# Softmax probabilities turned two quarters later, and the first two projection units interleaved without GpSimd

## The chip, the cores and the metric

The kernel runs on one core of a Trainium2 chip. The metric is the device time of one execution in microseconds; the median of three runs is compared. The engines are TensorE (PE: matmuls, and PEld: its weight loads), VectorE (DVE), ScalarE (ACT), GpSimd (POOL) and SyncE (SP, which here only issues DMAs).

## The reference

One layer over `x` of 512 tokens by 1024 channels, all in float32:

```python
proj = x @ w_in + b_in                     # 1024 -> 6728 columns, cut into
qa, fa, ia, za, qb, kb, vb, zb, qi, ki, wi, ga, gb = split(proj)
oa = rms_norm(hgrn2(qa, fa, ia)) * g       # gated linear recurrence, 4 heads of 128
# sparse attention, 8 heads of 64:
score = sum_h wi[h] * relu(qi[h] @ ki.T)   # 8 indexer heads, causal
keep  = top 128 keys of each query by score
p  = softmax(qb @ kb.T / 8 + t5_bias, over the kept keys)
ob = p @ vb
merged = sigmoid(ga) * ((oa * silu(za)) @ w_up_a) + sigmoid(gb) * ((ob * silu(zb)) @ w_up_b)
out = layer_norm(alpha * x + merged @ w_out)
```

## The kernel before

Every large product is done with split operands: `a = a_hi + a_lo` with `a_hi` rounded to the fp32r format, and `a*b` as three matmuls, hi·hi, hi·lo and lo·hi (`split_product`). The weights come in units of 256 columns (`UNITS`: kiwi, which holds ki and wi in 72 columns, then qi0, qi1, zb0 and so on up to up3, then four units of `w_out`). Unit u is loaded into `w_raw[:, u % 2]` by SP, rounded into `w_hi` by ScalarE (`split_hi`, two instructions of 128x1024), and subtracted into `w_lo` by GpSimd (`split_lo`, four pieces), or by VectorE for the units in `LO_DVE`, which counts them with a semaphore of its own.

TensorE works through the units in four quarters each. A quarter q = 4u + 0..3 of a normal unit is 12 matmuls of 512 columns (`quarter_f`), or 24 of 256 columns (`quarter_t`, for vb and ia). Two quarters fill one of the two projection banks; ScalarE or VectorE then copies the bank out (`leave_bank`), and TensorE waits for that copy before it fills the bank again a unit later. Behind each quarter every engine runs `side(q)`: the pieces of the token mixers that are due at that quarter. All engines are in-order, each with its program written in the order of q, so the order of all work is the order of these lists.

The softmax attention has 32 items (a block b of 128 queries, and a head), in pairs. `Q_ITEM` says at which quarter an item's scores are computed: quarters 39, 41, ... 53 for the first eight pairs, and 55, 56, 57, 59, 60, 61, 63, 64 for the last eight. For a pair due at q:

- TensorE `scores` in `side(q)` (L479) fills a log bank;
- VectorE `logits` in `side(q)` (L1042) adds the bias and the mask, and writes `prob` and the row maximum `nmax`; behind it in the same `side(q)` come the top-k rounds due then (L1018, L1019; rounds for block 3 are due at quarters 36 to 44), and behind these `invert_sums` (L1053);
- ScalarE `softmax_exp` and `normalise` in `side(q)` (L721, L729), the second waiting for the reciprocal of `invert_sums`;
- TensorE `turn_probs` in `side(q + 1)` (L488) transposes the probabilities; VectorE `move_probs` in `side(q + 1)` (L1030) copies them out; TensorE `attend` in `side(q + 2)` (L504) multiplies them with v; VectorE `gate_group` (L1064) takes a group of four items three quarters after its last item (`Q_GROUP`).

`prob` has two places, so `logits(i)` waits for the transposes of item i - 2.

The opening: ScalarE issues the load of the kiwi weights, then those of the biases and the identity, and rounds kiwi. VectorE makes `x_hi` and `x_lo` for each of the eight slices of x (`split_x`, L929 and L931). GpSimd subtracts kiwi's and unit 1's low parts. TensorE runs all of kiwi (24 matmuls, each slice when its x is there), then all of unit 1 (48). A ScalarE table load stands behind kiwi's copies (L670). SP loads the eight slices of x and then units 1, 2, ...; unit 2 waits until kiwi's low part is done, since they share a place. After the items comes the recurrence ("tree", L539 to L563); its first step on VectorE (`forget(0, 0)`, L1079) stands in `side(68)` behind the gates due by then.

Of the kernel before, what the change touches and what calls it, by code (L numbers as in the profile page):

```python
# [32 lines left out]
P = 128  # L33
# [9 lines left out]
UW = 256  # L43
# [36 lines left out]
Q_GROUP = [Q_ITEM[4 * n + 3] + 3 for n in range(len(GROUPS))]  # L80
# [3 lines left out]
LO_DVE = range(Q_PREP[0] // 4 + 1, Q_MERGE // 4 + 2)  # L84
# [14 lines left out]
def hybrid_kernel(nc, x_t, x_tok, w_units, w_kiwi, b_cols, b_ia, b_vb, lb_cols, g_cols, rel_bias,  # L99
                  ln_g, ln_b, one_hot, ident, causal, tree_masks, out):  # L100
    with ExitStack() as ctx:
# [16 lines left out]
        with ExitStack() as s:  # L118
# [9 lines left out]
            v_b = sb("v_b", [P, TB, D_B], stack=s)  # L128
            t5 = sb("t5", [P, HEADS_B, 2 * P], stack=s)
# [3 lines left out]
            prob = sb("prob", [P, 2, SEQ], stack=s)  # L133
# [33 lines left out]
        with ExitStack() as s:  # L167
# [16 lines left out]
        nmax = sb("nmax", [P, 2])  # L184
# [4 lines left out]
        proj_bank, log_bank, turn_bank, out_bank = ps[0:2], ps[2:4], ps[4:6], ps[6:8]  # L189
        up_bank = log_bank + turn_bank  # L190
# [8 lines left out]
            sem(n) for n in ("k_hi_done", "q_hi_done", "wi_done", "kiwi_out", "k_twice"))  # L199
        consts_in, table_in, row_out, t5_in = sem("consts_in"), sem("table_in"), sem("row_out"), sem("t5_in")  # L200
# [36 lines left out]
        def raw(u):  # L237
            w = unit_width(u)
            return w_raw[:, u % 2, 0:KT * w].rearrange("p (k n) -> p k n", k=KT)

        def split_target(u, over_x, ring):
# [4 lines left out]
            return ring[:, u % 2, :, 0:unit_width(u)]  # L246

        def wait_split_target(eng, u):

            gb3, up2, up3 = (UNITS.index(n) for n in ("gb3", "up2", "up3"))  # L250
            last = {NMAIN: gb3, NMAIN + 1: gb3, NMAIN + 2: up2, NMAIN + 3: up3}.get(u, u - 2)
            if last >= 0:
                eng.wait_ge(part_done, 2 * last + (2 if last else 1))

        def wait_lo(eng, u, n):

            if u in LO_DVE:
                eng.wait_ge(lo_dve, 4 * (u - LO_DVE[0]) + n)
# [87 lines left out]
        def _(sp):  # L346
            for k in range(KT):
                sp.dma_start(x_raw[:, k, :], x_t[:, k, :]).then_inc(x_in[k], 16)
            for u in range(1, NU):
                if u >= 2:  # L350
                    wait_lo(sp, u - 2, 4)
                unit = w_units[u - 1]
                for a in range(2):
                    c = slice(a * KT // 2 * UW, (a + 1) * KT // 2 * UW)
                    sp.dma_start(w_raw[:, u % 2, c], unit[:, c]).then_inc(w_in[u % 2][a], 16)
# [22 lines left out]
        def _(pe):  # L378
# [12 lines left out]
            def wait_bank(u, i):  # L391
                if u == 1 and i == 1:
                    pe.wait_ge(kiwi_out, 1)
# [3 lines left out]
            def quarter_f(u, i, j):  # L397

                bank = proj_bank[1 if UNITS[u] == "kiwi" else i]
                if j == 0:  # L400
                    wait_bank(u, i)
                c = slice(i * P, min(i * P + P, unit_width(u)))
                for k in range(4 * j, 4 * j + 4):
                    if i == 0:
                        wait_piece(u, k)
                    mm = split_product(bank[0:c.stop - c.start, :], w_hi[:, u % 2, k, c], w_lo[:, u % 2, k, c],
                                       x_hi[:, k, :], x_lo[:, k, :], k == 0, k == KT - 1)
                if j == 1:
                    mm.then_inc(part_done, 1)

# [13 lines left out]
            def turn_wi():  # L424
# [6 lines left out]
                mm.then_inc(part_done, 1)  # L431
# [50 lines left out]
            def turn_probs(i):  # L482
# [4 lines left out]
                for c in range(b + 1):  # L487
                    mm = nc.tensor.transpose(turn_bank[i % 2][:, queries(c)], prob[:, i % 2, queries(c)], id_sb[:])  # L488
# [86 lines left out]
            def side(q):  # L575

                if q == 4:
# [25 lines left out]
            for u, name in enumerate(UNITS):  # L603
                for q in range(4):
# [5 lines left out]
                    elif name != "kiwi" or i == 0:  # L610
                        quarter_f(u, i, j)
                    if (u, q) == (1, 3):
# [27 lines left out]
        def _(act):  # L640
            def round_tiles(u, k):
                nc.scalar.activation(split_target(u, x_hi, w_hi)[:, k, :], raw(u)[:, k, :],  # L642
                                     ACT.Copy).then_inc(hi_done, 1)

            def split_hi(u, a):

                if u == 0:
                    act.wait_ge(w_in[0][0], 16)
                else:
                    act.wait_ge(w_in[u % 2][a], 16 * (u // 2 + (a == 0 or u % 2)))  # L650
                if a == 0:
                    wait_split_target(act, u)
                round_tiles(u, slice(4 * a, 4 * a + 4))

            def leave_bank(u, i):
# [5 lines left out]
                act.wait_ge(part_done, 2 * u + i + 1)  # L661
# [837 lines left out]
```

## Time and profile before

| | us |
|---|---|
| median of three runs (509.02 to 511.66) | 510.69 |
| the profiled execution | 510.81 |
| its span, first to last instruction | 508.8 |
| PE busy in it | 479.8 (94%) |
| DVE busy | 294.3 (58%) |
| ACT busy | 206.4 (41%) |
| POOL busy | 187.6 (37%) |

The profiled execution lies 0.12 us from the median, so a sum made on it stands for the median too. Busy PE counts matmuls whose ends are modelled and overlap; the distance from one matmul's start to the next tells more.

### The profile page before, as it was taken

The numbers are of one execution on the slowest core, as the hardware profiler recorded it, in microseconds if no ns is written. First come the engines' busy times: TensorE is split into PE (matmuls) and PEld (weight loads), VectorE is DVE, ScalarE is ACT, GpSimd is POOL, SyncE is SP. The second block draws the span as 40 slices with busy tenths as digits, with TensorE's granted clock in tenths as the row PEclk, the third lists the DMA queues.
The fourth block names the chain that finished last, engine by engine and source line by source line (L and its number), as shares of the span: only waits on it lengthen the run. The fifth ranks groups of instructions, "written<-read, shape, count | busy, mean of one in ns | idle before, by whom it ended". The sixth has DMA issues, their size and how long they took to land. (4 is left out here: it accounts for less than half of the span.)

```text
span 508.8 us, 6785 instructions
## 1 busy us (share of the span) xinstructions
PE 479.8 (94%) x2566; PEld 387.9 (76%) x2566; DVE 294.3 (58%) x552; ACT 206.4 (41%) x343; POOL 187.6 (37%) x170
## 2 busy tenths in 40 slices
PE   4899999999779999999998899989999999999993
PEld 2578888889557888866787787868778888888882
DVE  6634589999773333343379967796352404264276
ACT  2444444323224533454375518545087333343000
POOL 2744433534335533663413200211005555686000
PEclk9899999999898999999999999999999999999998
DMA  8524222233021122112202202012205222348012
GB/s 307 200 85 165 84 83 84 82 107 134 9 83 29 56 84 84 43 41 84 80 4 84 83 1 84 22 63 82 84 0 166 82 84 82 112 166 303 1 62 103
DMA packets 15440, 45.69 MB, mean 90 GB/s; under 512 B 2056, under 2 KB 3504, under 8 KB 15408
## 3 DMA queue, kind: packets, MB, share of 16 engines
q1 hardware_dynamic: 14016, 44.06, 25.5%
q10 hardware_dynamic: 1392, 1.20, 0.7%
q8 instruction: 20, 0.33, 0.3%
q14 instruction: 12, 0.10, 0.1%
HBM read 43.14 MB, written 2.11 MB: 89 GB/s over the span
## 5 line engine op out<-in xcount | busy, mean ns | idle before, releaser
L1355 POOL TENSOR_TENSOR w_lo<-w_raw,w_hi 128x512 fp32r<-128x512 f32 (+1 forms) x104 | 135.2, 1326 | 153.1 <-ACT w_hi L642 153.1
L380 PE MATMUL bank<-x_hi,w_hi 128*128 128x512 f32 (+1 forms) x360 | 147.7, 410 | 9.4 <-POOL w_lo L1355 6.3
L381 PE MATMUL bank<-x_lo,w_hi 128*128 128x512 f32 (+1 forms) x360 | 143.1, 397 | 0.0
L382 PE MATMUL bank<-x_hi,w_lo 128*128 128x512 f32 (+1 forms) x360 | 142.8, 397 | 0.0
L380 PEld LDWEIGHTS bank<-x_hi,w_hi 128*128 128x128 f32 (+1 forms) x360 | 68.7, 191 | 31.7 <-POOL w_lo L1355 7.1
L382 PEld LDWEIGHTS bank<-x_hi,w_lo 128*128 128x128 f32 (+1 forms) x360 | 68.6, 191 | 15.9 <-issue 0.6
L381 PEld LDWEIGHTS bank<-x_lo,w_hi 128*128 128x128 f32 (+1 forms) x360 | 68.6, 191 | 13.5 <-issue 0.6
L642 ACT ACTIVATE w_hi<-w_raw 128x1024 fp32r<-128x1024 f32 (+1 forms) x66 | 66.7, 1033 | 14.7 <-DMA w_raw<-in_w_units 7.6
L721 ACT ACTIVATE prob<-prob,nmax 128x128 f32<-128x128 f32 (+3 forms) x32 | 17.8, 556 | 64.0 <-DVE nmax L1042 64.0
L380 PE MATMUL bank<-w_hi,x_hi 128*128 128x256 f32 x128 | 37.3, 291 | 0.0
L381 PE MATMUL bank<-w_lo,x_hi 128*128 128x256 f32 x128 | 36.2, 283 | 0.0
L382 PE MATMUL bank<-w_hi,x_lo 128*128 128x256 f32 x128 | 36.2, 283 | 0.0
L1042 DVE CUSTOM_DVE_ANT_0 prob<-bank,logit 128x128 f32<-128x128 f32 (+3 forms) x32 | 14.4, 489 | 33.1 <-PE bank L479 32.9
L1232 DVE TENSOR_TENSOR mix<-bank,gate_a 128x512 f32<-128x512 f32 x8 | 5.5, 692 | 41.7 <-PE bank L382 41.7
L339 POOL TENSOR_TENSOR dec<-cum 128x1024 f32<-128x1024 f32 x6 | 12.6, 2100 | 42.3 <-DVE k_c L1153 39.9
L1018 DVE MAX8 best<-score 128x8 f32<-128x256 f32 (+2 forms) x48 | 26.8, 558 | 1.0
L380 PEld LDWEIGHTS bank<-w_hi,x_hi 128*128 128x128 f32 x128 | 24.5, 191 | 3.2 <-issue 2.9
L1030 DVE COPY prob_t<-bank 128x128 f32<-128x128 f32 (+3 forms) x32 | 14.6, 489 | 20.8 <-PE bank L488 20.8
L1019 DVE MATCH_REPLACE8 score<-best,score 128x256 f32<-128x256 f32 (+2 forms) x48 | 26.1, 543 | 0.0
L1373 POOL TENSOR_TENSOR logit<-t,pen 128x256 f32<-128x256 f32 x24 | 17.5, 743 | 22.9 <-DVE nmax L1042 22.9
L380 PE MATMUL bank<-o_hi,w_hi 128*128 128x512 f32 x64 | 24.9, 389 | 0.0
L381 PE MATMUL bank<-o_lo,w_hi 128*128 128x512 f32 x64 | 24.9, 389 | 0.0
(161 smaller groups left out, 773.2 us busy)
## 6 DMA issues: line engine op xcount, KB each, us to landing
w_raw<-in_w_units SPq DMA_DIRECT2D x68, 512.0 KB, 4.6
x_raw<-in_x_t SPq DMA_DIRECT2D x8, 256.0 KB, 5.4
x_res<-in_x_tok SPq DMA_DIRECT2D x4, 512.0 KB, 7.2
out<-y_sb SPq DMA_DIRECT2D x8, 256.0 KB, 2.0
t_turned<-t_row SPq DMA_DIRECT2D x1, 1024.0 KB, 7.4
ln_gb<-in_ln_g SPq DMA_DIRECT2D x1, 512.0 KB, 6.7
ln_gb<-in_ln_b SPq DMA_DIRECT2D x1, 512.0 KB, 7.8
w_raw<-in_w_kiwi ACTq DMA_DIRECT2D x1, 288.0 KB, 4.2
```

Of the source, the lines that this page charges most:

```text
L339: return engine.tensor_tensor(groups(dec[:, lv % 2, :], h), c, c[:, :, h - 1:h].broadcast_to([P, 2 * SEQ // (2 * h), 2 * h]), ALU.subtract)
L380: nc.tensor.matmul(dst, a_hi, b_hi, start=first, stop=False)
L381: nc.tensor.matmul(dst, a_hi, b_lo, start=False, stop=False)
L382: return nc.tensor.matmul(dst, a_lo, b_hi, start=False, stop=last)
L642: nc.scalar.activation(split_target(u, x_hi, w_hi)[:, k, :], raw(u)[:, k, :], ACT.Copy).then_inc(hi_done, 1)
L721: nc.scalar.activation(prob[:, i % 2, 0:n], prob[:, i % 2, 0:n], ACT.Exp, bias=nmax[:, i % 2:i % 2 + 1], scale=-1.0, accum_out=prob_sum[:, ...
L1018: link(nc.vector.max(best8[:], score[b][:]))
L1019: link(nc.vector.match_replace(score[b][:], best8[:], score[b][:], TAKEN))
L1030: nc.vector.tensor_copy(prob_t[:, i % 4, 0:n], turn_bank[i % 2][:, 0:n]).then_inc(turn_out[i % 2], 1)
L1042: nc.vector.tensor_tensor_reduce(out=prob[:, i % 2, 0:n], in0=log_bank[i % 2][:, 0:n], in1=logit[:, i % 2, 0:n], scale=-1.0, scalar=3e38, ...
L1355: nc.gpsimd.tensor_tensor(split_target(u, x_lo, w_lo)[:, k, :], raw(u)[:, k, :], split_target(u, x_hi, w_hi)[:, k, :].bitcast(F32), ALU.su ...
L1373: nc.gpsimd.tensor_tensor(logit[:, i % 2, n - band:n], t5[:, h, 2 * P - band:], pen[b][:, n - band:] if b else causal_sb[:], ALU.add).then ...
```

## The change

Probabilities: `prob` and `nmax` get four places; `turn_probs` and `move_probs` move from q + 1 to q + 2, `attend` from q + 2 to q + 3, and `gate_group` from + 3 to + 4. Opening: kiwi gets its own three tiles; ScalarE rounds x as well as kiwi and units 1 and 2; VectorE does all subtractions of units 0 and 1 (they join `LO_DVE`); TensorE interleaves kiwi with unit 1, kiwi into bank `out_bank[0]`; unit 1's halves are loaded between slices of x, and unit 2 without a wait. The transposes of wi move from quarter 4 to 8, the T5 table's matmul from 7 to 9, and its copy from 7 to 10. The table load stands first on ScalarE.

```diff
-Q_GROUP = [Q_ITEM[4 * n + 3] + 3 for n in range(len(GROUPS))]
+Q_GROUP = [Q_ITEM[4 * n + 3] + 4 for n in range(len(GROUPS))]
-LO_DVE = range(Q_PREP[0] // 4 + 1, Q_MERGE // 4 + 2)
+LO_DVE = (0, 1) + tuple(range(Q_PREP[0] // 4 + 1, Q_MERGE // 4 + 2))
+                kiwi_raw = sb("kiwi_raw", [P, KT, WKI], stack=s2)
+                kiwi_hi, kiwi_lo = (sb(n, [P, KT, WKI], F32R, s2) for n in ("kiwi_hi", "kiwi_lo"))
-            prob = sb("prob", [P, 2, SEQ], stack=s)
+            prob = sb("prob", [P, 4, SEQ], stack=s)
-        nmax = sb("nmax", [P, 2])
+        nmax = sb("nmax", [P, 4])
+        kiwi_bank = out_bank[0]
...
# SyncE
             for k in range(KT):
                 sp.dma_start(x_raw[:, k, :], x_t[:, k, :]).then_inc(x_in[k], 16)
-            for u in range(1, NU):
-                if u >= 2:
+                if k == 1:
+                    load_half(1, 0)
+                if k == 4:
+                    load_half(1, 1)
+            for u in range(2, NU):
+                if u >= 3:
                     wait_lo(sp, u - 2, 4)
...
# TensorE
+            def opening():
+                def kiwi(k):
+                    wait_piece(0, k)
+                    return split_product(kiwi_bank[0:WKI, :], kiwi_hi[:, k, :], kiwi_lo[:, k, :],
+                                         x_hi[:, k, :], x_lo[:, k, :], k == 0, k == KT - 1)
+                def first_qi(i, k):
+                    wait_piece(1, k)
+                    c = slice(i * P, i * P + P)
+                    return split_product(proj_bank[i][:], w_hi[:, 1, k, c], w_lo[:, 1, k, c],
+                                         x_hi[:, k, :], x_lo[:, k, :], k == 0, k == KT - 1)
+                for k in range(3):
+                    kiwi(k)
+                for k in range(KT // 2):
+                    if k == 2:
+                        kiwi(3)
+                    first_qi(0, k)
+                    first_qi(1, k)
+                for k in range(KT // 2, KT):
+                    done = kiwi(k)
+                    if k < KT - 1:
+                        first_qi(0, k)
+                done.then_inc(part_done, 1)
+                first_qi(0, KT - 1).then_inc(part_done, 1)
+                for k in range(KT // 2, KT):
+                    done = first_qi(1, k)
+                done.then_inc(part_done, 1)
...
-                for i in items_at(q - 2)[::2]:
+                for i in items_at(q - 3)[::2]:
                     attend(i)
-                for i in items_at(q - 1):
+                for i in items_at(q - 2):
                     turn_probs(i)
                 for i in items_at(q):
                     scores(i)
...
# ScalarE
-                    nc.scalar.preload_act_table_set("sigmoid_and_others")     # behind kiwi's copies
...
+            nc.scalar.preload_act_table_set("sigmoid_and_others")
+            act.dma_start(kiwi_raw[:].rearrange("p k n -> p (k n)"), w_kiwi).then_inc(kiwi_in, 16)
             act.dma_start(bias[:], b_cols).then_inc(early_in, 16)
             act.dma_start(id_sb[:], ident).then_inc(early_in, 16)
             split_hi(0, 0)
+            round_x(0)
             split_hi(0, 1)
+            round_x(1)
+            round_x(2)
+            split_hi(1, 0)
+            round_x(3)
+            round_x(4)
+            split_hi(1, 1)
+            for k in range(5, KT):
+                round_x(k)
+            split_hi(2, 0)
+            split_hi(2, 1)
             act.dma_start(rel_sb[:], rel_bias).then_inc(table_in, 16)     # the constants' loads follow
...
# VectorE
             def split_x(k):
-                dve.wait_ge(x_in[k], 16)
-                nc.vector.tensor_copy(x_hi[:, k, :], x_raw[:, k, :]).then_inc(x_hi_done, 1)
                 dve.wait_ge(x_hi_done, k + 1)
...
-                if i >= 2:
-                    dve.wait_ge(turn_full, i - 1)
+                if i >= 4:
+                    dve.wait_ge(turn_full, i - 3)
...
-                for i in items_at(q - 1):
+                for i in items_at(q - 2):
                     move_probs(i)
...
-            for k in range(KT):
-                split_x(k)
+            split_lo(0, 0)
+            split_x(0)
+            split_lo(0, 1)
+            split_x(1)
+            split_lo(0, 2)
+            split_lo(0, 3)
+            split_x(2)
+            split_lo(1, 0)
+            split_x(3)
+            split_lo(1, 1)
+            split_x(4)
+            split_lo(1, 2)
+            split_x(5)
+            split_x(6)
+            split_lo(1, 3)
+            split_x(7)
...
# GpSimd
-            for u in (0, 1):
-                for j in range(4):
-                    split_lo(u, j)
```

## Rows read from the trace of the kernel before

**Rows 1.** The page: busy us (share of the span) xinstructions.

```profile
PE 479.8 (94%) x2566; PEld 387.9 (76%) x2566; DVE 294.3 (58%) x552; ACT 206.4 (41%) x343; POOL 187.6 (37%) x170
```

**Rows 2.** Waits of PE, whole span: us in total, times, longest us.

```profile
PE bank L488 <- ACT prob L729: 6.6, 6, 2.8
PE bank L380 <- POOL w_lo L1355: 6.3, 1, 6.3
...
PE bank L380 <- DVE x_lo L931: 2.4, 2, 2.1
```

**Rows 3.** Windows: length, busy us (xinstructions) of each engine, PEclk, DMA, GB/s.

```profile
133.46:136.87 3.41, 3.01 (x8) 2.42 (x9) 2.43 (x6) 2.53 (x4) 1.75 (x2) 0.51 0.02 5
...
153.94:157.35 3.41, 3.41 (x10) 2.52 (x8) 1.99 (x5) 1.36 (x2) 2.92 (x3) 0.51 0.00 0
17.41:20.82 3.41, 3.41 (x10) 2.65 (x9) 0.88 (x2) 3.31 (x4) 1.32 (x2) 0.51 0.27 74
```

**Rows 4.** Timeline of PE, opening: start us, us, instruction [idle before, releaser].

```profile
9.61 0.63 PE L381 MATMUL bank<-x_lo,w_hi 128*72 128x512 f32 x1
...
10.04 0.63 PE L382 MATMUL bank<-x_hi,w_lo 128*72 128x512 f32 x1
...
16.40 0.46 PE L380 MATMUL bank<-x_hi,w_hi 128*72 128x512 f32 x1 [2.11 <-DVE x_lo L931]
...
21.59 0.41 PE L429 MATMUL bank<-id_sb,score 8*128 8x8 f32 x4
...
29.78 0.39 PE L381 MATMUL bank<-x_lo,w_hi 128*128 128x512 f32 x1
30.00 0.39 PE L382 MATMUL bank<-x_hi,w_lo 128*128 128x512 f32 x1
```

**Rows 5.** Timeline of ACT and its queue, opening.

```profile
2.14 1.28 ACT L642 ACT_TABLE_LOAD   x1 [2.14 <-issue]
...
4.99 0.44 ACT L642 ACTIVATE w_hi<-w_raw 128x288 fp32r<-128x288 f32 x1 [1.57 <-DMA w_raw<-in_w_kiwi]
5.00 0.34 ACTq L863 DMA_DIRECT2D rel_sb<-in_rel_bias  x1
```

**Rows 6.** Groups by form: busy us, mean ns of one, idle before.

```profile
L642 ACT ACTIVATE w_hi<-w_raw 128x1024 fp32r<-128x1024 f32 x64 | 65.9, 1051 | 13.1 <-DMA w_raw<-in_w_units 7.6 <-PE bank L382 5.5
...
L825 ACT ACTIVATE m_hi<-mix 128x512 fp32r<-128x512 f32 x8 | 5.0, 630 | 23.2 <-DVE mix L1236 23.2
```

**Rows 7.** Tile x_raw: ns min/median/max, first and last start us.

```profile
L931 DVE TENSOR_TENSOR x_lo<-x_raw,x_hi x8: 691/693/1631, 5.2 to 14.7; 128x512 fp32r<-128x512 f32 x8
```

**Rows 8.** DMA view of 0 to 40 us: GB/s in 40 slices of 1 us.

```profile
GB/s 0 0 94 233 212 364 290 392 404 404 388 403 421 411 400 382 413 415 413 407 393 341 14 0 0 0 87 322 240 415 322 11 0 0 0 0 0 0 22 0
```

**Rows 9.** Timeline of PE, quarters 39 to 45.

```profile
127.65 0.49 PE L479 MATMUL bank<-k_b,q_b 64*128 64x128 f32 x4
...
133.86 0.77 PE L488 MATMUL bank<-id_sb,prob 128*128 128x128 f32 x2 [2.77 <-ACT prob L729]
...
158.18 0.70 PE L479 MATMUL bank<-k_b,q_b 64*128 64x256 f32 x4
```

**Rows 10.** Timeline of DVE, quarters 39 to 41.

```profile
133.20 0.17 DVE L1053 RECIPROCAL prob_rcp<-prob_sum 128x2 f32<-128x2 f32 x1
...
139.36 0.29 DVE L1042 CUSTOM_DVE_ANT_0 prob<-bank,logit 128x128 f32<-128x128 f32 x1 [3.02 <-PE bank L479]
```

**Rows 11.** Groups by form: the first instruction of a top-k round, 512 columns.

```profile
L1018 DVE MAX8 best<-score 128x8 f32<-128x512 f32 x16 | 11.1, 691 | 0.3
```

**Rows 12.** Window of DVE alone, 68 to 133 us.

```profile
68.00:133.00 65.00, 60.97 (x147) 1.00 0.24 81
```

**Rows 13.** Timeline around the last items: PE, then DVE.

```profile
250.19 1.09 PE L504 MATMUL bank<-prob_t,v_b 128*64 128x128 f32 x16
...
251.36 0.42 DVE L1064 TENSOR_TENSOR z_b<-bank,z_b 128x256 f32<-128x256 f32 x1 [2.97 <-PE bank L504]
255.09 1.23 DVE L1079 SCALAR_TENSOR_TENSOR dec<-cum 128x1024 f32<-128x1024 f32 x1 [3.31 <-ACT q_a L703]
```

More of the change, by code:

```diff
@@ L237, in raw, with split_target @@
         def raw(u):
-            w = unit_width(u)
-            return w_raw[:, u % 2, 0:KT * w].rearrange("p (k n) -> p k n", k=KT)
-        def split_target(u, over_x, ring):
+            return kiwi_raw if u == 0 else w_raw[:, u % 2, :].rearrange("p (k n) -> p k n", k=KT)
+        def split_target(u, kiwi, over_x, ring):
+            if u == 0:
+                return kiwi
             if NMAIN <= u < NMAIN + 2:
@@ L245, in split_target @@
                 return over_x[:, :, c:c + UW]
-            return ring[:, u % 2, :, 0:unit_width(u)]
+            return ring[:, u % 2, :, :]
         def wait_split_target(eng, u):
@@ L405, in quarter_f @@
                         wait_piece(u, k)
-                    mm = split_product(bank[0:c.stop - c.start, :], w_hi[:, u % 2, k, c], w_lo[:, u % 2, k, c],
+                    mm = split_product(proj_bank[i][:], w_hi[:, u % 2, k, c], w_lo[:, u % 2, k, c],
                                        x_hi[:, k, :], x_lo[:, k, :], k == 0, k == KT - 1)
@@ L575, in side @@
             def side(q):
-                if q == 4:
+                if q == 8:
                     turn_wi()
@@ L601, in t5_table @@
                                  stop=True).then_inc(table_full, 1)
-            for u, name in enumerate(UNITS):
+            opening()
+            for u, name in list(enumerate(UNITS))[2:]:
                 for q in range(4):
@@ L609, in _ @@
                         quarter_t(u, i, j)
-                    elif name != "kiwi" or i == 0:
+                    else:
                         quarter_f(u, i, j)
-                    if (u, q) == (1, 3):
+                    if (u, q) == (2, 1):
                         t5_table()
@@ L875, in _ @@
                     leave_bank(u - 1, 1)
-                elif j == 2:
+                elif j == 2 and u >= 1:
                     leave_bank(u, 0)
-                if u >= 1 and j < 2:
+                elif q == 7:
+                    leave_bank(0, 0)
+                if u >= 2 and j < 2:
                     split_hi(u + 1 + (u == NMAIN - 1), j)
@@ L984, in leave_bank, with scale_w @@
                                                    op0=ALU.add, op1=ALU.mult).then_inc(proj_out[i], 1)
[L985 to L993 removed]
+            def scale_w():
+                dve.wait_ge(wi_turned, 1)
+                nc.vector.tensor_scalar(
+                    w_idx[:], turn_bank[0][:, 0:TB * HEADS_I].rearrange("p (t h) -> p t h", t=TB),
+                    WSCALE, None, ALU.mult).then_inc(w_idx_done, 1)
             def add_score(i):
@@ L1253, in side @@
                     leave_bank(u - 1, 1)
-                if j == 2:
+                if j == 2 and u >= 1:
                     leave_bank(u, 0)
+                if q == 7:
+                    leave_bank(0, 0)
                 for i in range(2 * (q - Q_DOTS), 2 * (q - Q_DOTS) + 2):
@@ L1268, in side @@
                     invert_sums(i)
-                if u + 1 in LO_DVE:
+                if u and u + 1 in LO_DVE:
                     for piece in ((), (0,), (1, 2), (3,))[j]:
```

84 lines of the change are left out of this document (42 added, 42 removed).

## The prediction, written before the changed kernel ran

> **What bounds the kernel now.** I read the page first: PE is busy 94% of the span, no other engine above 58% [rows 1]. So a microsecond is gained only where PE stands still or runs slowly. The waits of PE name the places [rows 2]: 6.6 us for the normalised probabilities, 6.3 us for GpSimd's low part of kiwi and 2.4 us for x_lo in the opening, and all the others lie in the recurrence, where the change moves nothing in PE's list. The first 6.3 us is PE's start, since nothing ran before.
>
> The windows give a second loss [rows 3]. In three stretches of 3.41 us the granted clock is 0.51, that is the 1.2 GHz level. Each starts behind a wait of PE: the first behind the 2.11 us for the last slice of x [rows 4], the second behind the 2.77 us for the first transpose [rows 9], the third behind the wait of a later pair. A 512-column matmul follows its predecessor by 0.22 to 0.23 us at full clock (29.78 to 30.00) and by 0.43 us at the start (9.61 to 10.04) [rows 4], so such a stretch does half its work and costs 3.41 / 2 = 1.7 us. The trace has no record of a reduced clock before 10.5 us, but the pitch of 0.43 us there is that of the low level; I take PE's first 4.1 us of work (6.3 to the end of that slot, 10.5) as slow in both kernels.
>
> **The opening.** Before, unit 1's last matmul starts at 30.00 and ends its slot at 30.23 [rows 4]. Four transposes of wi stand inside, 0.41 us [rows 4], and the change moves them behind this point, so the comparable end is 29.8.
>
> After, I walk the lists. ScalarE: kiwi's weights land at 4.99 and half of them is rounded in 0.44 us [rows 5]; a slice of x takes 0.63 us and a half unit 1.05 us [rows 6]. Landings: by the rates of each microsecond, 0.8 MB are there at 5.0 and 0.4 MB follow per us [rows 8]. In the new order of SP (two slices of x 0.52 MB, half a unit 0.52, three slices 0.79, half a unit 0.52, three slices 0.79, then unit 2), with 0.39 MB of kiwi, bias and identity beside it, the first half unit is there at 6.6, the third slice at 7.2, the second half unit at 9.8, the last slice at 11.8 and unit 2 at 14.4. ScalarE then ends x0 at 6.0, kiwi's second half 6.5, x1 7.1, x2 7.8, unit 1's first half 8.9, x3 and x4 10.1, its second half 11.2, the last x at 13.0, unit 2 at 15.6. VectorE needs 0.69 us for each subtraction [rows 7], a third of that (an estimate from the width, 144 of 512 columns) for kiwi's: x_lo 0 at 6.8, x_lo 1 at 7.9, x_lo 2 at 9.0, unit 1's first piece 9.7, second 11.0, third 12.3, last x_lo 15.0. Its eight roundings of x are gone, and with GpSimd silent until unit 2 at 14.4 the longest x_lo of 1.63 us [rows 7] should not come back before the last slice.
>
> PE: first matmul at 6.8 instead of 6.3 (kiwi's first piece was on GpSimd and x rounded on VectorE in parallel; now x waits behind kiwi on ScalarE). It does kiwi's three slices at 0.43 us a matmul until 10.6; x_lo 2 and unit 1's first piece are each there before. The clock rises about 10.9. Of 72 matmuls some 9.7 are then done; the other 62.3 take 62.3 x 0.228 = 14.2 us, and each later piece is 3 us or more ahead of them. End 25.1. Gain 29.8 - 25.1 = 4.7; I take 4.5, since the two engines' handovers of about 0.1 us fall in the first steps. Bounds: 5.2 if the first matmul starts at 6.3 as before, and 2.5 if the three slices of kiwi don't bridge to unit 1 and a gap of 2 us opens (the one that was there before, 2.11).
>
> What is late next: q_hi and q_lo of unit 1 leave the banks by 25 (part 0) and 28 (part 1), with k and wi between; PE wants bank 0 at 25.1 and bank 1 at 30.6. VectorE has for both some 5 instructions of 0.7 us. Wi's transposes wait for wi until about 25 and stand at 27.8: covered. Unit 2's low part is on GpSimd from 14.4 to about 20: covered. The T5 copy stands later by three quarters, behind a matmul that moved two; SP holds unit 4's load behind it, which lands at about 37 against PE's want at 48. The constants' loads are issued at 15.6 and wanted after 35. Each of these costs nothing, and each would cost at most its own length, under 1 us.
>
> **The probabilities.** The pair of quarter 39 has its scores at 127.65; at the end of quarter 40 PE waits until 133.86 [rows 9]. The wait is not for ScalarE itself but for the reciprocal at 133.20 [rows 10], and that is late because two top-k rounds stand between logits and reciprocal, each of a search (0.69 us [rows 11]) and a replacement as wide, with small gaps and a value load 1.5 us, so 3.0 us. VectorE is 94% busy from 68 to 133 us (60.97 of 65.00) [rows 12]: it is late by its load, and no order on PE makes it faster. It doesn't have to be: after the stall it sits idle itself for 3.02 us until PE's next scores [rows 10]. Both waited for each other in turn.
>
> With the transposes a quarter later PE does 12 matmuls (2.74 us) more before it asks. The scores take 0.4, so from 128.1 on 24 matmuls x 0.228 end at 133.6, and the transposes can start at 133.86 as before: 0.2 us of wait in place of 2.77. Then the next pair's scores come at once (134.3) instead of 4.9 us later, and VectorE goes on without its idle time. For the next pair: VectorE does a bank copy, a round, the move and the logits until 136.4, two rounds until 139.4, the reciprocal, and ScalarE has normalised by 140.4; PE asks at 140.7. The third: normalised from 147.6 to 148.0, PE asks at 147.7. From quarter 45 on no rounds are due. Over these six quarters VectorE's work is about 20 us against PE's 20.7 (six times 2.74, and 1.4 us for transposes, scores and products in every second one). The scores of quarter 45 come at about 148.5 instead of 158.18 [rows 9].
>
> As a sum: the waits of 6.6 us [rows 2] leave 0.3, and the two slow stretches [rows 3] go, 2 x 1.7 = 3.4. Gain 6.6 - 0.3 + 3.4 = 9.7 us. Bounds: 10.4, if in addition the gaps that the waits view does not count around the six go; and 6.0, if the balance is 1 us worse in each of the first two pairs and one slow stretch stays (9.7 - 2 - 1.7). Below this the rival with the closed loop begins.
>
> The queues moved past: move_probs now stands ahead of the next pair's logits on VectorE in the same quarter, 0.5 us for 128-column items and 1.3 for 512; PE's bank for the scores is free long before. The copies of the projection banks on ScalarE stand behind normalise: PE wants the bank of quarter 46 at about 149.3, the copy starts at 148.0 and takes 0.7. That cover is 0.6 us, the thinnest of all.
>
> **The last pair.** Its product with v was over at 251.3, four instructions of VectorE's path before it mattered [rows 13]. Now it stands in side(67), behind qa0's last matmul. That ends at about 254.3: VectorE was released at 255.09 by the copy of its bank, some 0.7 us long. The product takes 1.09, the gate 0.42, and only then comes the first step of the recurrence, 255.8 instead of 255.09 [rows 13]; rounded for overlap, 0.65 us later. VectorE sets the pace of that stage. Bounds 0 (if a later wait on ScalarE swallows it) and 1.3 (if GpSimd's reset mask, which waits for the same product, is late too).
>
> **The sum** on the profiled execution: 510.8 - 4.5 - 9.7 + 0.65 = 497.3 us. It is 0.1 from the median of before, so this is the forecast.
>
> **The table load.** In the trace it came behind three DMA issues on ScalarE's queue and took 1.28 us, and at 5.00 a DMA was issued from that queue while a rounding that stands before it ran [rows 5]. So the issue does not wait for ScalarE's arithmetic; whether it waits for a table load no row shows. If it does, kiwi lands 1.28 us later and so does everything to 25.1.
> The Trainium skill, page "ScalarE: Activation LUTs", section "What ACT_TABLE_LOAD costs", gives about 1283 ns for the load and as much as 1380 ns more for a drain ahead of it; the first agrees with the trace's 1.28, and with both the opening would begin 2.7 us late and the sum would be 500.0.
>
> **Rivals.**
> A. The DMA issues wait behind the first table load: 497.3 + 1.3 = 498.6 us. For: it is first in the list and engine queues are in order. Against: the issue at 5.00. 15%.
> B. VectorE is the bound of 68 to 156 us and gives nothing back: PE's wait only moves from the transposes to the next thing that VectorE must finish. Then only the opening's gain and half of the rest come: 510.8 - 4.5 - 5 + 0.65 = 502. For: 94% busy. Against: VectorE's own idle time of 3.02, and more in the next pairs. 13%.
> C. Slower: the closed loop. In quarter q + 2 PE now has the transposes of one pair ahead of the scores of the next, and VectorE the move ahead of the logits. So scores, logits, rounds, reciprocal, normalise, transposes and next scores form one ring, of 0.5 + 0.5 + 3.0 + 0.2 + 0.7 + 0.5 = 5.4 us and VectorE's backlog, against PE's 6.9 us for two quarters. If the backlog makes it longer, every pair stalls and each stall over 2 us brings a slow stretch of 1.7. From 13.5 / 8 = 1.7 us a pair over the first eight pairs the change loses; with 2 us and the slow stretch, 8 x 3.7 = 29.6 come against a gain of 4.5 in the opening and of 10 in the old waits: 526 us. Against: only three of the pairs have rounds in the ring. 3%.
>
> **How the numbers follow.** Forecast 66%, A 15%, B 13%, C 3%, and 3% that several covers fail together and the time stays about 510. The forecast's own range is 495 to 499.5; to hold 8 in 10 I reach down to 494.8 (510.8 - 5.2 - 10.4, and nothing lost at the last pair, is 495.2) and up to 502, which takes in A and the centre of B. A difference of 0.5% (2.6 us) is about what can be told from no change: faster 0.94, same 0.03, slower 0.03.
>
> **What would show it.** Right: no wait of PE over 0.5 us between its first matmul and 250 us; unit 1 done near 25; the granted clock at its high level from about 11 us to the end; scores of quarter 45 near 144 (148.5 less the opening's gain); VectorE's longest wait for L479 under 1 us at quarter 41. Wrong: kiwi's landing near 6.3 (A); a wait at L488 or L380 in 125 to 150 us with a clock of 0.5 behind it (B, C); a later first L1079 than one quarter-67 product would explain.

## The result, and the profile after

The changed kernel takes 497.34 us (median of four runs, 495.9 to 498.88); the kernel before, with one more run, 509.96 us. The ratio is 0.9749, 95% interval 0.9708 to 0.9791. The forecast was 497.3. It was worked out from 510.8, a gain of 13.5 us; against 509.96 the gain is 12.6 us. The profiled execution took 497.14 us with a span of 495.3, 13.5 us less than before.

The page: busy time by engine, then the granted clock of TensorE in 40 slices.

```profile
PE 474.5 (96%) x2566; PEld 386.5 (78%) x2566; DVE 287.8 (58%) x552; ACT 209.5 (42%) x350; POOL 178.6 (36%) x162
...
PEclk9999999999999999999999999999999999999998
```

PE is busy 5 us less than in [rows 1] with the same 2566 matmuls: nothing was taken out of its list, but fewer ran slowly. The waits of PE answer to [rows 2]:

```profile
PE bank L396 <- DVE x_lo L989: 7.7, 2, 6.4
PE bank L588 <- DVE att L1241: 3.1, 2, 1.9
PE bank L582 <- DVE k_c L1212: 1.5, 2, 0.8
```

The 6.6 us for the probabilities are gone entirely. Of the opening's 7.7 us, 6.4 is the start and 1.3 a new wait. The recurrence's are as they were. The first two pairs and the fourth, on PE's timeline (L522 the scores, L531 the transposes), answer to [rows 9]:

```profile
125.22 0.49 PE L522 MATMUL bank<-k_b,q_b 64*128 64x128 f32 x4
...
131.43 0.62 PE L531 MATMUL bank<-id_sb,prob 128*128 128x128 f32 x2
131.98 0.49 PE L522 MATMUL bank<-k_b,q_b 64*128 64x128 f32 x4
...
138.58 0.38 PE L531 MATMUL bank<-id_sb,prob 128*128 128x128 f32 x2
...
146.23 0.70 PE L522 MATMUL bank<-k_b,q_b 64*128 64x256 f32 x4
```

The transposes have no idle time in front of them. From the scores of quarter 39 to those of quarter 45 it is 21.0 us instead of 30.5. The stretch that answers to the first of [rows 3], in a window view, now has a clock of 1.00:

```profile
133.46:136.87 3.41, 3.41 (x18) 2.47 (x17) 3.27 (x11) 0.98 (x5) 3.41 (x4) 1.00 0.00 0
```

Where the 13.5 us of the two profiles came from, read at three marks (before, then after):

| mark on a timeline | before | after | gained up to there |
|---|---|---|---|
| scores of quarter 39 | 127.65 | 125.22 | 2.4 |
| scores of quarter 45 | 158.18 | 146.23 | 12.0 |
| first step of the recurrence on VectorE | 255.09 | 241.76 | 13.3 |
| span | 508.8 | 495.3 | 13.5 |

### The profile page after: what moved, and what is told of

The parts are those of the page before. It is cut to its first block and busy times, and to the rows that moved or that the text cites. A ratio compares the mean times of both kernels' runs of the same rounds, so it can differ in the third digit from the quotient of the medians.

```text
span 495.3 us, 6784 instructions
## 1 busy us (share of the span) xinstructions
PE 474.5 (96%) x2566; PEld 386.5 (78%) x2566; DVE 287.8 (58%) x552; ACT 209.5 (42%) x350; POOL 178.6 (36%) x162
## 5 line engine op out<-in xcount | busy, mean ns | idle before, releaser
L1433 POOL TENSOR_TENSOR w_lo<-w_raw,w_hi 128x512 fp32r<-128x512 f32 x96 | 126.4, 1342 | 159.1 <-ACT w_hi L686 159.1
L396 PE MATMUL bank<-x_hi,w_hi 128*128 128x512 f32 x352 | 142.2, 404 | 0.1
L397 PE MATMUL bank<-x_lo,w_hi 128*128 128x512 f32 x352 | 137.9, 392 | 0.0
L398 PE MATMUL bank<-x_hi,w_lo 128*128 128x512 f32 x352 | 137.7, 391 | 0.0
L396 PEld LDWEIGHTS bank<-x_hi,w_hi 128*128 128x128 f32 x352 | 66.4, 189 | 19.7 <-issue 5.4
L398 PEld LDWEIGHTS bank<-x_hi,w_lo 128*128 128x128 f32 x352 | 66.4, 189 | 14.6
L397 PEld LDWEIGHTS bank<-x_lo,w_hi 128*128 128x128 f32 x352 | 66.5, 189 | 13.0 <-issue 0.5
L686 ACT ACTIVATE w_hi<-w_raw 128x1024 fp32r<-128x1024 f32 x64 | 66.0, 1052 | 8.1 <-PE bank L398 5.5
L1089 DVE COPY prob_t<-bank 128x128 f32<-128x128 f32 (+3 forms) x32 | 14.2, 486 | 40.1 <-PE bank L531 40.0
L349 POOL TENSOR_TENSOR dec<-cum 128x1024 f32<-128x1024 f32 x6 | 12.6, 2100 | 42.3 <-DVE k_c L1212 39.9
L398 PE MATMUL bank<-o_hi,w_lo 128*128 128x512 f32 x64 | 24.9, 389 | 0.0
L397 PEld LDWEIGHTS bank<-w_lo,x_hi 128*128 128x128 f32 x128 | 24.5, 191 | 0.0
```

The source lines that it names most:

```text
L349: return engine.tensor_tensor(groups(dec[:, lv % 2, :], h), c, c[:, :, h - 1:h].broadcast_to([P, 2 * SEQ // (2 * h), 2 * h]), ALU.subtract)
L396: nc.tensor.matmul(dst, a_hi, b_hi, start=first, stop=False)
L397: nc.tensor.matmul(dst, a_hi, b_lo, start=False, stop=False)
L398: return nc.tensor.matmul(dst, a_lo, b_hi, start=False, stop=last)
L686: nc.scalar.activation(split_target(u, kiwi_hi, x_hi, w_hi)[:, k, :], raw(u)[:, k, :], ACT.Copy).then_inc(hi_done, 1)
L1089: nc.vector.tensor_copy(prob_t[:, i % 4, 0:n], turn_bank[i % 2][:, 0:n]).then_inc(turn_out[i % 2], 1)
```

## The experiments

All are timed against the kernel before on the same chip. A run's last column is its profiled span times its mean granted clock: what the span would be if PE's time at 1.2 GHz had cost nothing. The opening is left out of this: the row of 10.5 to 14 us below shows a granted clock of 1.00 where matmuls follow at half pitch. The product is a way to set profiles beside each other that caught different stretches of low clock (before: 508.8 x 0.987 = 502.2; the changed kernel: 495.3 x 0.997 = 493.8). The mean clocks have three digits, so 0.3 us either way.

| kernel | median us | ratio to before, 95% | span, clock | span x clock |
|---|---|---|---|---|
| e1 opening alone | 507.65 | 0.9963 (0.9939 to 0.9986) | 506.1, 0.989 | 500.5 |
| e2 probabilities alone | 502.75 | 0.9845 (0.9804 to 0.9885) | 497.6, 0.993 | 494.1 |
| e3 both, two places | 503.95 | 0.9872 (0.983 to 0.9915) | 502.1, 0.988 | 496.1 |
| e4 both, turned at q + 1 | 506.41 | 0.9942 (0.9918 to 0.9965) | 506.6, 0.990 | 501.5 |
| e5 before, reciprocal between rounds | 503.03 | 0.9879 (0.9846 to 0.9912) | 501.1, 0.993 | 497.6 |
| e6 third slice of x first | 495.53 | 0.9745 (0.9703 to 0.9786) | 496.5, 0.989 | 491.0 |
| e7 four slices of x first | 495.66 | 0.9745 (0.9705 to 0.9785) | 493.8, 0.996 | 491.8 |
| e8 the changed kernel again | 497.33 | 0.9791 (0.9738 to 0.9844) | 494.2, 0.997 | 492.7 |
| e9 e6 and e5's edit | 494.84 | 0.9724 (0.9696 to 0.9751) | 492.5, 0.996 | 490.5 |
| e10 small loads late | 497.45 | 0.978 (0.9732 to 0.9827) | 499.0, 0.988 | 493.0 |
| e11 rows of 2048 bytes | 497.97 | 0.9789 (0.974 to 0.9839) | 495.9, 0.997 | 494.4 |

### The two halves by themselves: e1 and e2

e1 is the changed kernel with `Q_GROUP`, `attend`, `turn_probs` and `move_probs` one quarter earlier again and two places. e2 is the kernel before with the edits for the probabilities, of which two are:

```diff
-                for i in items_at(q - 1):
+                for i in items_at(q - 2):
                     turn_probs(i)
...
-            prob = sb("prob", [P, 2, SEQ], stack=s)
+            prob = sb("prob", [P, 4, SEQ], stack=s)
```

> The new opening with the probabilities as before (two places, transposes a quarter later). My theory, parts that add: the changed kernel's trace gives the opening 2.4 us (scores of quarter 39 at 125.21 instead of 127.65), so 510 - 2.4 = about 507.5, with the 2.8 us wait for the first transpose and both slow stretches of TensorE's clock back in 130 to 158 us. Rival, parts that help each other (the earlier opening only pays because the later transposes let it through, or the reverse): within 0.5 us of 510, or well under 505.

> The opening as before, the probabilities with four places and turned two quarters behind. My theory: 11 us less than before, 499, scores of quarter 45 about 9.5 us earlier than 158.2, no wait at the transposes and no reduced clock after 21 us. Rival (part of these 11 us came from VectorE starting its loaded stretch earlier after the new opening): 501 or more, with a wait left at the first transposes.

e1 measured 507.65, as the additive theory had it (507.5), but the kernel before took 509.18 on this chip: the opening alone is worth 1.5 us at the median (0.7 to 3.1 by the interval) and 1.7 by span times clock, where 2.4 was expected. In its profile the waits of PE have the whole old group back:

```profile
PE bank L531 <- ACT prob L777: 6.6, 6, 2.8
```

But the two slow stretches that I had expected behind them in 130 to 158 us were not there. This execution had one stretch of 6.8 us somewhere else, in the recurrence, as its windows show (the clock stands third from the end):

```profile
280.00:285.00 5.00, 5.00 (x18) 4.33 (x17) 4.93 (x9) 4.01 (x8) 0.00 (x0) 0.50 0.48 155
285.00:290.00 5.00, 5.00 (x28) 4.41 (x27) 0.93 (x3) 2.00 (x4) 1.90 (x1) 0.82 0.13 55
```

e2's profile has no wait for the probabilities and its scores of quarter 45 at 148.51, 9.7 us earlier than before, as expected. Its profiled run took 499.59 at a mean clock of 0.993, but the other three took 502.7 to 502.8 at 0.984 to 0.985. So the expected 499 is one of its runs and the median is 502.75; the rival's 501 is met by the time but not by its sign, a wait left at the transposes. The waits of PE in e2:

```profile
PE bank L380 <- POOL w_lo L1355: 6.2, 1, 6.2
PE bank L545 <- DVE att L1182: 3.1, 2, 1.9
```

By ratios the halves give 0.37% and 1.55%, 1.9% together, and both in one kernel 2.1% (e8) to 2.5% (the first result), with intervals of 0.25 to 0.5 points on each side. Span times clock has 8.1 us for the probabilities on the old opening (502.2 to 494.1), and 6.7 to 7.8 on the new one (500.5 to 493.8 or 492.7). So the two are additive as far as this can tell; the interacting theory has nothing for it.

### Places or order: e3 and e4

e3 takes the changed kernel back to two places, e4 takes it back to transposes at q + 1 and keeps four.

```diff
-                if i >= 4:
-                    dve.wait_ge(turn_full, i - 3)
+                if i >= 2:
+                    dve.wait_ge(turn_full, i - 1)
```

> The changed kernel, but prob and nmax have two places again, so that logits of a pair wait for the transposes of the pair before. My theory: over the first eight pairs nothing changes (pairs two quarters apart, transposes stand ahead of the next scores), over the last eight, due at 55, 56, 57, 59 and so on, logits wait up to a quarter and VectorE's and TensorE's lists hold each other: some of pairs 56, 57, 60, 61, 64 wait 1 to 3 us, 3 to 8 us in all, 500 to 505. Rival (the order alone is the gain, the places are cover): 497.

> The changed kernel, but transposes one quarter behind, as before, with four places kept. My theory (the wait was for the reciprocal behind two top-k rounds, not for a place): as the kernel with the new opening alone, 507.5, the wait of 2.8 us and both slow stretches back. Rival (the two places were what made VectorE late, since its logits waited for transposes): 500 or less.

e4: the wait is back at the same place and of the same length as before, on PE's timeline at quarter 40:

```profile
131.98 0.77 PE L531 MATMUL bank<-id_sb,prob 128*128 128x128 f32 x2 [2.77 <-ACT prob L777]
```

With 506.41 it is within the interval of e1, so four places alone bring nothing that can be measured. e3 was expected at 500 to 505 and took 503.95; its first eight pairs keep the new order's pace, and in the last eight VectorE's logits wait for transposes. The waits of VectorE for PE from 185 to 245 us (L1101 are the logits, L1089 is `move_probs`), first in e3, then in the changed kernel:

```profile
DVE prob L1101 <- PE bank L531: 22.9, 5, 5.9
DVE prob_t L1089 <- PE bank L531: 8.5, 4, 4.5
```

```profile
DVE prob_t L1089 <- PE bank L531: 21.3, 9, 4.5
...
DVE prob L1101 <- PE bank L522: 6.5, 4, 2.4
```

With one more of 3.0 us in the changed kernel, at the last gate, VectorE waits as long for PE in both, 31.4 and 30.8 us. What differs is that in e3 the logits are among what waits for transposes, and PE then waits in its turn, in these lines of e3's waits of PE from 185 to 245 us, of which the changed kernel has none:

```profile
PE bank L522 <- DVE nmax L1101: 1.0, 2, 0.6
PE bank L547 <- DVE prob_t L1089: 0.7, 1, 0.7
```

The last pair's scores come at 230.64 in e3 and at 227.80 in the changed kernel, 2.8 us later, of which 0.5 was there at quarter 39; the other 2.3 is the price of two places (by span times clock too, 496.1 against 493.8). That is less than the 3 to 8 us that I expected. The median fell into 500 to 505 with the help of low clock: all four runs of e3 have a mean clock of 0.988 to 0.989, three of the changed kernel's four 0.996 or 0.997, and why e3's is the lower in every run stays open. The order brings the gain, and the places keep it where pairs follow at one quarter's distance.

### Load or order on VectorE: e5

```diff
-                for b, r in rounds.get(q, ()):
+                due = rounds.get(q, ())
+                for b, r in due[:1]:
                     topk_round(b, r)
                 for i in items_at(q)[::2]:
                     invert_sums(i)
+                for b, r in due[1:]:
+                    topk_round(b, r)
```

> The kernel before, with one edit on VectorE: the reciprocal of the sums stands between the two top-k rounds of its quarter instead of behind both. My theory (the place of the reciprocal behind two rounds made the wait at the transposes): the reciprocal of the first pair comes about 1.4 us sooner (131.9 instead of 133.2), each of the three long waits shrinks by about 1.4 us, 2.8 to 1.4 and the others to near 0, 4 us less waiting and fewer slow stretches: 505 or less. Rival (VectorE's load is the bound, the order is not): the waits only move, 508 to 510.

It took 503.03, 6.3 us under the kernel before (4.6 by span times clock), from one step moved within its quarter, on an engine that is 94% busy from 68 to 133 us. Its first transposes on PE's timeline, and all waits for the probabilities in its waits of PE:

```profile
132.10 0.62 PE L488 MATMUL bank<-id_sb,prob 128*128 128x128 f32 x2 [1.25 <-ACT prob L729]
```

```profile
PE bank L488 <- ACT prob L729: 2.2, 5, 1.2
```

2.77 became 1.25, as expected, and 6.6 became 2.2. VectorE does the same work (busy 294.5 us against 294.3), so its load was not what held PE back. Rival B of the prediction falls.

### The opening's order of loads: e6, e7 and e8

```diff
             for k in range(KT):
                 sp.dma_start(x_raw[:, k, :], x_t[:, k, :]).then_inc(x_in[k], 16)
-                if k == 1:
+                if k == 2:
                     load_half(1, 0)
```

e7 has `k == 3` there and all four kiwi products ahead of unit 1's, with the lists of ScalarE and VectorE to match.

> The changed kernel with one edit in the loads: the third slice of x is issued ahead of the first half of unit 1, not behind it. My theory (TensorE's gap at 9.2 us and the late rise of its clock come from that slice's landing at 9.0): the slice lands by 7.5, the gap of 1.33 us is gone, but unit 1's first half is 0.7 us later, which ends at about 10.5 and opens a gap under 0.7 us; the scores of quarter 39 come 0.5 to 2.5 us sooner than 125.2. Rival (the clock rises when it does whatever the gap, and only the order of the waits changes): within 0.5 us of 125.2.

> The changed kernel with four slices of x ahead of unit 1's first half, and all four of their kiwi products ahead of unit 1's, ScalarE's and VectorE's lists in that order too. My theory: four slices of kiwi are 5.1 us of slow matmuls, from 6.4 to 11.5, and unit 1's first piece is ready at about 11; no gap over 0.3 us, the clock rises near 10.5 instead of 14, and the scores of quarter 39 come 3 us sooner, at about 122. Rival (unit 1's half lands so late that a gap opens behind kiwi): a gap of 1 us or more at 11.5, and 124 to 126.

> The changed kernel itself, beside the others on one chip. Median 497 to 499. My theory on the spread of its runs: where a run has a stretch of low clock in the recurrence it is 3 us longer; the gap of 1.3 us in the opening is in this profile too. Rival: the gap was one run's accident and is not there.

First the opening of the changed kernel, on ScalarE's timeline (its queue's DMA issues are ACTq) and then on PE's:

```profile
0.73 1.28 ACT L906 ACT_TABLE_LOAD   x1 [0.73 <-PEq L1567]
...
0.76 0.39 ACTq L907 DMA_DIRECT2D kiwi_raw<-in_w_kiwi  x1
...
4.89 0.61 ACT L702 ACTIVATE x_hi<-x_raw 128x512 fp32r<-128x512 f32 x1
6.10 0.63 ACT L702 ACTIVATE x_hi<-x_raw 128x512 fp32r<-128x512 f32 x1 [0.27 <-DMA x_raw<-in_x_t]
9.01 0.63 ACT L702 ACTIVATE x_hi<-x_raw 128x512 fp32r<-128x512 f32 x1 [2.28 <-DMA x_raw<-in_x_t]
```

```profile
6.37 0.67 PE L396 MATMUL bank<-x_hi,kiwi_hi 128*72 128x512 f32 x1 [6.37 <-DVE x_lo L989]
...
8.55 0.63 PE L398 MATMUL bank<-x_hi,kiwi_lo 128*72 128x512 f32 x1
...
10.52 0.67 PE L396 MATMUL bank<-x_hi,kiwi_hi 128*72 128x512 f32 x1 [1.33 <-DVE x_lo L989]
...
13.97 0.44 PE L398 MATMUL bank<-x_hi,w_lo 128*128 128x512 f32 x1
14.25 0.39 PE L396 MATMUL bank<-x_hi,w_hi 128*128 128x512 f32 x1
...
27.02 0.39 PE L398 MATMUL bank<-x_hi,w_lo 128*128 128x512 f32 x1
```

ScalarE starts to round the third slice at 9.01, PE waits 1.33 us for it, and the pitch of its matmuls stays at 0.43 until 13.97, where it falls to 0.23 to 0.28. The 72nd and last matmul of kiwi and unit 1 starts at 27.02 and ends its slot at 27.25. The granted clock does not show the low pitch, so that here it has to be read from the starts of the matmuls. The window of 10.5 to 14 us:

```profile
10.50:14.00 3.50, 3.48 (x9) 2.54 (x10) 3.38 (x6) 3.50 (x7) 0.00 (x0) 1.00 1.05 416
```

e8 has the same gap (1.43 us, ending at 10.75), so it is no accident; but there the pitch is 0.27 and less at once behind it. Now e6, on PE's timeline:

```profile
9.32 0.63 PE L396 MATMUL bank<-x_hi,kiwi_hi 128*72 128x512 f32 x1
...
10.60 0.60 PE L396 MATMUL bank<-x_hi,w_hi 128*128 128x512 f32 x1
...
11.52 0.39 PE L396 MATMUL bank<-x_hi,w_hi 128*128 128x512 f32 x1
11.74 0.40 PE L397 MATMUL bank<-x_lo,w_hi 128*128 128x512 f32 x1
```

No gap, full pitch from 11.03, and the scores of quarter 39 at 123.21, 2.0 us sooner than in the changed kernel's first profile and 0.9 sooner than in e8's (124.09). The median is 495.53 against e8's 497.33 on the same chip, where the two intervals overlap. I had expected a small gap between kiwi and unit 1 in its place; there was none. e7 removes the gap as well, but its scores come at 123.61, not at 122: the kiwi products moved forward bring no more once the gap is closed.

All profiles with the new opening together: with a gap ahead of the third slice (0.76 to 1.66 us) the low pitch lasted until 14.0 to 15.7 us in five (the changed kernel, e3, e4, e10, e11) and was over right behind the gap in two (e1, e8). Without a gap (e6, e7, e9) it lasted until 10.5 to 11.8. The scores of quarter 39 go by this: 125.2 to 125.8 us in the five, 124.8 and 124.1 in the two, 122.9 to 123.6 in the last three. e10, with the shortest gap of all, is among the latest, so when the low pitch ends weighs more than the gap's length. That a gap is followed by a late rise is seen in five of seven profiles; why it isn't in the other two stays open.

Part of the late landing is the rate. The window of 4.5 to 6 us, first in the changed kernel, then in e6 (the last column is GB/s):

```profile
4.50:6.00 1.50, 0.00 (x0) 0.00 (x0) 0.77 (x2) 1.29 (x3) 0.00 (x0) 1.00 0.92 215
```

```profile
4.50:6.00 1.50, 0.00 (x0) 0.00 (x0) 0.43 (x2) 1.11 (x3) 0.00 (x0) 1.00 1.10 392
```

The DMA engines are 92% busy in the first, at half the rate. The rest is the order in which loads land. The windows before and behind it in the changed kernel, with 78 GB/s from 0 to 3 us:

```profile
3.00:4.50 1.50, 0.00 (x0) 0.00 (x0) 0.00 (x0) 0.00 (x0) 0.00 (x0) 1.00 1.02 344
...
6.00:7.50 1.50, 1.13 (x3) 0.56 (x3) 1.18 (x4) 0.63 (x1) 0.00 (x0) 1.00 0.97 335
7.50:9.00 1.50, 1.50 (x4) 0.67 (x3) 0.39 (x2) 0.00 (x0) 0.00 (x0) 1.00 1.05 389
```

Everything issued up to and with the third slice is 1.70 MB (kiwi and the small loads 0.39, three slices 0.79, half a unit 0.52). By these rates that much had moved at 7.8 us, but the slice was there only at 9.0, when 2.16 MB had moved: loads issued behind it had been served meanwhile. In the six other profiles with this order the same sum is 1.0 to 2.1 us ahead of the landing. In e6, with the slice third, its 1.18 MB had moved at 5.9 us and ScalarE has rounded it by 7.2.

### Why the rate falls: e10 and e11

e10 issues the biases and the identity behind x's roundings. e11 loads unit 1's first half in two DMAs:

```diff
-                sp.dma_start(w_raw[:, u % 2, c], w_units[u - 1][:, c]).then_inc(w_in[u % 2][a], 16)
+                parts2 = (c,) if (u, a) != (1, 0) else (slice(0, c.stop // 2), slice(c.stop // 2, c.stop))
+                for c in parts2:
+                    sp.dma_start(w_raw[:, u % 2, c], w_units[u - 1][:, c]).then_inc(w_in[u % 2][a], 16)
```

> The changed kernel, with the loads of the biases (128 rows of 248 bytes) and the identity (128 rows of 512 bytes) issued behind all of x's roundings. It asks what makes the DMA rate fall to 195 to 258 GB/s from 4.5 to 6 us in the four profiles where unit 1's half follows the second slice of x, against 341 to 392 in the five others. Theory S (the small rows, which the same engines carry just then): the rate is above 340, the third slice lands a microsecond sooner and the gap is gone. Theory W (the rows of 4096 bytes themselves, when they come this early): the rate stays under 260, the gap stays.

> The changed kernel with unit 1's first half loaded in two DMAs of 256 KB with rows of 2048 bytes, in the same place behind the second slice of x. Theory W (rows of 4096 bytes bring the rate down from 4.5 to 6 us): the rate is above 340 GB/s, the third slice of x lands under 8.3 us and the gap ahead of its products is under 0.7 us. Rival (the weights' place in memory or their place in the order, whatever the rows): under 260 GB/s, a gap of 0.7 to 1.4 us as before.

The same window of e10, then of e11:

```profile
4.50:6.00 1.50, 0.00 (x0) 0.00 (x0) 0.62 (x2) 1.31 (x4) 0.00 (x0) 1.00 0.99 262
```

```profile
4.50:6.00 1.50, 0.00 (x0) 0.00 (x0) 0.67 (x2) 1.35 (x4) 0.00 (x0) 1.00 0.98 214
```

e10's gap is 0.76 us and e11's 1.66. So the small rows are at most a part of it (theory S fails: 262, not 340), and rows of 4096 bytes are not the cause (theory W fails: 214). What is left is that a half unit of weights stands third in the queue. Whether its place in the order or its place in memory makes that slow was not tested, and the cause stays open.

### The best version: e9

It is e6 with e5's edit.

> The changed kernel with both edits that helped: the third slice of x ahead of unit 1's first half, and the reciprocal between the two top-k rounds. My theory (with the transposes two quarters behind nothing waits for the reciprocal any more): no gain over the loads' edit alone, 495.5, within 1 us. Rival (VectorE's and TensorE's lists still hold each other somewhere between 125 and 150 us): 494 or less.

494.84 us, all four runs between 494.35 and 495.31, ratio 0.9724 (0.9696 to 0.9751): the fastest kernel here, though its lead over e6 (0.9745) is inside the intervals. Within 1 us, as expected, so at most a small wait was left: from the scores of quarter 39 to those of 45 it is 20.6 us in e9 against 21.1 in e6.

## Why the prediction was right, and where it was off

**The time** came out at the forecast by luck: two terms were off in opposite directions, each beyond its own bounds, and met. The opening gave 2.4 us in this profile (forecast 4.5, bounds 2.5 to 5.2), the probabilities 11.5 (forecast 9.7, bounds 6.0 to 10.4). With 0.6 lost at the last pair and 0.2 won behind it that is the 13.5 us.

**The wait at the transposes: right.** The prediction said 6.6 us would leave 0.3, by order and not by load. After, the waits view shows none; e5 shows the mechanism from the other side (an earlier reciprocal alone takes 4.4 of the 6.6 us away), and e4 shows that the places had no part in it.

**The pace of the six quarters: right.** Scores of quarter 45 were forecast 9.7 us earlier relative to those of 39 (148.5 against 158.18); they came 9.5 earlier (21.0 against 30.5 us). Up to the last pair's scores another 1.6 us came (241.36 to 227.80 in all), for which the sum had only the three short waits inside its 6.6, and 0.3 more by ScalarE's copy of qa0 (254.26 to 240.36). So the term was mis-sized by 1.4 to 1.8 us, and what gave the rest is not shown.

**The slow stretches: right in this profile, not a fixed price.** I counted 2 x 1.7 us as gone for certain. Both are gone in the changed kernel. But e1 and e4 have the same waits as before; e1 had no slow stretch behind them, and e4 one of double length (mean clock 0.58 from 130 to 138 us). Such a stretch also came in the recurrence, where no edit changed a wait, in e1, e3, e6 and e10 and in none of the other nine profiles. And 3 of 49 further runs of the kernel before have a mean clock of 0.996 and a span of 504.0 to 504.1 us: even there the stretches need not come. The changed kernel's runs at 0.996 or 0.997 have 494.1 to 496.1, so some 8 to 10 us are won without them. So the term is a chance of 1.7 to 3.4 us per long wait, not a sum. It also makes runs of one kernel differ: e2's 499.59 against 502.8.

**The opening: the mis-sized term.** Forecast 4.5 us, bounds 2.5 to 5.2; measured 2.4 at the scores of quarter 39, and in e1, e3, e4 and e8, which have the same opening, 2.9, 1.9, 1.9 and 3.6 (124.77, 125.71, 125.77 and 124.09 against 127.65). The step that failed is the landing of the third slice: "the third slice at 7.2" was 9.01. I took 0.4 MB per us and landing in the order of issue for granted, in an order of loads that no trace had shown. The rate was 215 GB/s for 1.5 us, which turns 7.2 into 7.8; the other 1.2 us is that loads issued behind the slice were served before it was complete. (The rates of [rows 8] are slices of 0.75 us, since that view covers 0 to 30 us and not 0 to 40. With slices of 0.75 us they add up to the 0.8 MB at 5.0 us that I used.) The late landing made the gap of 1.33 us, which I had named as the lower bound's mechanism, though between the wrong pieces. The second step that failed is "the clock rises about 10.9": the low pitch lasted until 14.0, as in four other profiles with the gap, but not in e1 and e8. As a sum against the end of unit 1, forecast at 25.1 and measured at 27.25: 3.1 us more at half pitch are 1.5; the gap lies inside the slow time and left out some 3 matmuls, 0.7 us at full pitch; the first matmul at 6.37 instead of my 6.8 gives one back, 0.2. That is 2.0 of the missing 2.15.

**The last pair: right.** The recurrence's first step on VectorE began 0.83 us after ScalarE's copy of qa0 before (255.09 - 254.26) and begins 1.40 after it now, 0.57 later where 0.65 was forecast. PE's, ScalarE's and VectorE's timelines there:

```profile
240.25 1.09 PE L547 MATMUL bank<-prob_t,v_b 128*64 128x128 f32 x16
```

```profile
240.36 0.69 ACT L751 ACTIVATE q_a<-bank,bias 128x512 f32<-128x512 f32 x1 [6.05 <-PE bank L398]
```

```profile
241.41 0.42 DVE L1123 TENSOR_TENSOR z_b<-bank,z_b 128x256 f32<-128x256 f32 x1 [2.97 <-PE bank L547]
241.76 1.22 DVE L1138 SCALAR_TENSOR_TENSOR dec<-cum 128x1024 f32<-128x1024 f32 x1
```

The wait for the product (2.97) is now the one that sets that step; in [rows 13] the same wait stood there with 3.3 us to spare.

**Rivals.** A, the DMA issues behind the table load, is refuted by the timeline above: the load runs from 0.73 to 2.01 and kiwi's DMA is issued at 0.76. The Trainium skill ("ScalarE: Activation LUTs", "What ACT_TABLE_LOAD costs") has the load at 1283 ns, as here (1.28), and about 1380 ns of drain with it for every switch to a different set. That drain is not in this trace. At 362.49 the changed kernel switches from the logarithm's set to the sigmoid's, on ScalarE's timeline:

```profile
361.43 1.04 ACT L686 ACTIVATE w_hi<-w_raw 128x1024 fp32r<-128x1024 f32 x1
362.49 1.28 ACT L948 ACT_TABLE_LOAD   x1
363.79 1.06 ACT L954 ACTIVATE o_hi<-z_a 128x1024 fp32r<-128x1024 f32 x1
```

The load stands 0.02 us behind the instruction ahead of it and the next one 0.02 us behind the load, so a switch costs 1.3 us here and the measurement decides: the prediction's 500.0 with the drain has nothing for it here. B, VectorE's load, is refuted by e5. C, the closed ring, did not come: no pair waits.

**The signs.** Scores of quarter 45 near 144 came at 146.23 and unit 1 was done at 27.25 instead of near 25, both late by the opening's 2 us. "No wait of PE over 0.5 us" before 250 us is broken by the gap of 1.33. The granted clock is high to the end but for the last 3.4 us; every profile here ends in such a stretch, of 3 to 6 us, so it takes nothing from the comparison. VectorE's wait for the scores at quarter 41 is gone, as foretold.

## What to carry to other kernels

When an engine waits for a result of a loaded engine, look at what stands between that result and its inputs in the loaded engine's list before you call it the bound: here moving one reciprocal ahead of one top-k round was worth 6.3 us of the median (4.6 by span times clock), and asking a quarter later was worth all of the wait. More buffers buy nothing until the order lets them be used, and are then what keeps the order alive where items come closely. In an opening, the order in which loads are issued is worth testing by itself, since neither the bytes nor the mean rate told which slice would be late. And a time that meets its forecast says little until each term is read at its own mark.

## What the runs showed of the hardware that was not expected

A wait of PE of 2.77 us was followed by a stretch at 1.2 GHz in the kernel before (3.41 us) and in e4 (6.8 us), and by none in e1, with the same waits. Stretches of 6.8 us came in the recurrence in four of the profiles, without a change to the waits there. One profile's slow stretches are not a property of the kernel, and 1.7 to 3.4 us of difference between two profiles can be this alone.

In the opening the granted clock reads 1.00 where 512-column matmuls follow at 0.43 us, the pitch of 1.2 GHz (10.5 to 14 us of the changed kernel). With a gap of 0.76 to 1.66 us ahead of the third slice the low pitch lasted until 14.0 to 15.7 us in five profiles of seven, without one until 10.5 to 11.8 in all three.

With a half unit of weights third in the load queue, the DMA rate from 4.5 to 6 us is 195 to 262 GB/s in all seven profiles that have that order, and 341 to 392 in the others, with the engines 89% or more busy in all of them. With that order a 256 KB slice issued behind it landed 1.0 to 2.1 us after the bytes up to and with it had moved, in these seven profiles.
